# Head norms run inside the next mixer's projection; Hyena's weights, filter taps and one DeltaNet load are rearranged

## The reference, cut to what matters

```python
def head_rmsnorm(o, w, n_heads):
    b_, l_, hd = o.shape
    oh = o.reshape(b_, l_, n_heads, hd // n_heads)
    oh = oh * lax.rsqrt(jnp.mean(oh * oh, axis=-1, keepdims=True) + EPS)
    return oh.reshape(b_, l_, hd) * w.astype(F32)
# GLA and DeltaNet: y = head_rmsnorm(o, norm_w, 4) * silu(og)
# Mamba:            y = head_rmsnorm((o + xs * d) * silu(z), norm_w, 4), then back to row-major order

def hyena_filters(l_, w1, b1, w2, b2, w3, b3, w4, freq):
    ...                                         # feats: (1024, 33)
    h = jnp.sin(f[0] * (feats @ w1 + b1))       # 64 wide
    h = jnp.sin(f[1] * (h @ w2 + b2))
    h = jnp.sin(f[2] * (h @ w3 + b3))
    h = h @ w4                                  # 1024 wide: 2 orders x 2 directions x 256 channels
    ...
    return h.reshape(l_, HY_ORDER, N_DIR, D_GROUP) * window[:, None, None, :]
```

## Time and profile before

| | us |
|---|---|
| median of 3 runs (2051.81 to 2055.04) | 2052.24 |
| the profiled execution | 2053.32 |
| its span in the trace | 2051.5 |
| PE busy | 1722.3 (84% of the span) |
| DVE busy | 1141.3 (56%) |
| ACT busy | 850.6 (41%) |
| POOL busy | 363.4 (18%) |
| TensorE clock granted, mean | 0.908 of full |

### The profile page before, as it was taken

One profiled execution on the slowest core, in us unless ns is written; L12 is line 12 of the kernel. 1 busy time (PEld: TensorE's weight loads), 2 busy tenths in 40 slices (PEclk: granted clock), 3 DMA queues, 4 the chain that ended last, 5 costly groups with the idle time before them and its releaser, 6 DMA issues. The chain is left out here.

```text
span 2051.5 us, 20519 instructions
## 1 busy us (share of the span) xinstructions
PE 1722.3 (84%) x7806; PEld 1228.2 (60%) x7806; DVE 1141.3 (56%) x1325; ACT 850.6 (41%) x1115; POOL 363.4 (18%) x455
## 2 busy tenths in 40 slices
PE   5898979975897849969899888970999999999981
PEld 2453745465455638954335656860888888888860
DVE  3621842268224535654323343337888888888874
ACT  4112224311224626632200003431777777777752
POOL 0000310031000578300041342430010101010100
PEclk9899989988898869979879999985999999999996
DMA  9620200020000733320142024213999999999955
GB/s 370 237 100 1 83 0 0 0 83 1 0 1 4 243 119 99 104 81 0 42 128 103 0 82 155 69 54 156 368 381 400 383 399 379 402 383 403 379 218 184
DMA packets 105706, 338.26 MB, mean 165 GB/s; under 512 B 35050, under 2 KB 44829, under 8 KB 80905
## 3 DMA queue, kind: packets, MB, share of 16 engines
q1 hardware_dynamic: 97024, 314.28, 40.4%
q0 software_dynamic: 4608, 16.78, 3.3%
q10 hardware_dynamic: 3977, 5.90, 1.0%
HBM read 303.83 MB, written 33.09 MB: 164 GB/s over the span
## 5 line engine op out<-in xcount | busy, mean ns | idle before, releaser
L2842 DVE TENSOR_TENSOR w_lo<-w_raw,w_hi 128x2048 fp32r<-128x2048 f32 x192 | 438.4, 2291 | 66.0 <-ACT w_hi L2788 66.0
L2788 ACT ACTIVATE w_hi<-w_raw 128x2048 fp32r<-128x2048 f32 x192 | 368.0, 1917 | 143.6 <-PE ps L2744 134.9
L489 PE MATMUL ps<-hT,w_mixer 128*128 128x512 f32 (+1 forms) x768 | 311.2, 566 | 5.6 <-PEq L186 4.7
L489 PEld LDWEIGHTS ps<-hT,w_mixer 128*128 128x128 f32 x768 | 146.8, 193 | 161.4 <-issue 158.1
L2742 PE MATMUL ps<-w_hi,xsT_hi 128*128 128x512 f32 x512 | 203.1, 397 | 2.4 <-DVE xsT_lo L2847 2.4
L2744 PE MATMUL ps<-w_hi,xsT_lo 128*128 128x512 f32 x512 | 200.5, 392 | 0.0
L2743 PE MATMUL ps<-w_lo,xsT_hi 128*128 128x512 f32 x512 | 200.4, 391 | 0.0
L2717 POOL DMA_INDIRECT moe_sum<-y,idx_col x16 | 32.0, 1998 | 490.6 <-ACT y L2808 490.6
L2742 PEld LDWEIGHTS ps<-w_hi,xsT_hi 128*128 128x128 f32 x512 | 96.8, 189 | 22.1 <-DVE xsT_lo L2847 2.8
L2744 PEld LDWEIGHTS ps<-w_hi,xsT_lo 128*128 128x128 f32 x512 | 96.7, 189 | 20.5
L2743 PEld LDWEIGHTS ps<-w_lo,xsT_hi 128*128 128x128 f32 x512 | 96.8, 189 | 19.4
(11 more groups left out here) (473 smaller groups left out, 2990.1 us busy)
## 6 DMA issues: line engine op xcount, KB each, us to landing
w_raw<-in_moe_w_gate SPq DMA_DIRECT2D x64, 1024.0 KB, 6.8
w_raw<-in_moe_w_up SPq DMA_DIRECT2D x64, 1024.0 KB, 8.6
w_raw<-in_moe_w_down SPq DMA_DIRECT2D x64, 1024.0 KB, 8.5
w_mod_row<-in_w_mod SPq DMA_DIRECT2D x32, 512.0 KB, 5.1
w_mod<-in_w_mod SPq DMA_DIRECT2D x8, 1024.0 KB, 14.5
w_mixer<-in_w_in SPq DMA_DIRECT2D x4, 2048.0 KB, 10.6
dn_ma<-dn_ma SPq DMA_DIRECT2D x16, 512.0 KB, 3.3
dn_mT<-dn_ma SPq DMA_DIRECT2D x20, 256.0 KB, 3.7
```

The lines of the kernel that those rows point to most:

```text
L489: last = nc.tensor.matmul(S.ps[:, 3 * (i % 2) + c, 0:n], S.w[:, k, b["col"]:b["col"] + P], S.hT[:, k, t0:t0 + n], start=(k == 0), stop=(k ...
L2788: nc.scalar.activation(wh[q % RING][:, :], S.raw[q % RAW][:, :], ACT.Copy).then_inc(s.hi, 1)
L2842: nc.vector.tensor_tensor(wl[q % RING][:, :], S.raw[q % RAW][:, :], wh[q % RING][:, :].bitcast(F32), ALU.subtract).then_inc(s.lo, 1)
```

## The change

The three head norms are no longer stages. `HeadNorm` gives its pieces to the next `project_conv`: ACT's silu and root come first on ACT, DVE's chain comes first on DVE, POOL's multiplication after the memsets, and PE's 16 transposes come after block 0 of the projection, into four banks of their own, with ACT's four copies after its copies of block 0. PE waits for a bank's copy before it writes that bank again (`free`). `o` and the squares lie in parts of `yT` that are not yet in use, so that the next mixer's buffers don't overlap them.

Hyena's weights are no longer loaded beside the norm of DeltaNet but at the start of `hy_c`, in four transfers of two row groups each, and PE's first product waits for them one at a time. The filter layers are computed twice, on partitions 0 to 63 and 64 to 127, and `w4` is split between the two halves, so that the two tap matmuls of a token tile read different halves of the array's rows. One DVE instruction multiplies both orders by the window (128x1024), DVE takes the sum and POOL only the difference, each 128x512; the window comes in four transfers; the table `hy_fwd` is waited for only by the stage that reads it. In DeltaNet, `dn_a` ends after 8 small loads; the other 8 are issued at the start of `dn_s`. Fewer stages move the two clearings of semaphores from before `dn_c` and `hy_c` to before `dn_l` and `hy_f`.

```diff
-def project_conv(nc, S, A, name, blocks, plan, ctx=True, side=None):
+def project_conv(nc, S, A, name, blocks, plan, norm, ctx=True, side=None, weights=None):
...
+            if weights:
+                col, n = weights
+                src = A["w_in"][0, :, col:col + n].rearrange("(p k) n -> p k n", p=P)
+                for j in range(4):
+                    sp.dma_start(S.w[:, 2 * j:2 * j + 2, 0:n], src[:, 2 * j:2 * j + 2, :]).then_inc(s.w_in[j], 16)
...
             last.then_inc(s.zeroed, 1)
+            norm.pool(s, pool)
...
                 if n >= 2:
                     pe.wait_ge(s.tok_e, n - 1)
+                norm.free(s, pe, 6 + n % 2)
...
-            pe.wait_ge(S.w_ready, S.w_count)
+            if not weights:
+                pe.wait_ge(S.w_ready, S.w_count)
...
+                    if i >= 1:
+                        norm.free(s, pe, 3 * (i % 2) + c)
                     for k in range(KD):
+                        if weights and i == 0 and c == mine[0][0] and k % 2 == 0:
+                            pe.wait_ge(s.w_in[k // 2], 16)
                         last = nc.tensor.matmul(S.ps[:, 3 * (i % 2) + c, 0:n], S.w[:, k, b["col"]:b["col"] + P],
...
                     to_tokens(pe, i - 1)
+                if i == 0:
+                    norm.pe(s, pe)
                 if side:
...
         def _(act):
+            norm.act(s, act)
             act.wait_ge(s.zeroed, 1)
...
                     nc.scalar.activation(d, src, ACT.Copy).then_inc(s.evac, 1)
+                if i == 0:
+                    norm.act_out(s, act)
...
+            norm.dve(s, dve, ch)
             for i, b in enumerate(blocks):
...
+    def pe(self, s, pe):
+        S = self.S
+        pe.wait_ge(s.nsq, 1)
+        for g in range(4):
+            kb, half = g // 2, g % 2
+            for t in range(4):
+                last = self.nc.tensor.transpose(S.ps[:, self.banks[g], t * P:(t + 1) * P],
+                                                self.o[:, half * 4 + t, kb * P:(kb + 1) * P], S.t("ident"))
+            last.then_inc(s.ntr, 1)
+
+    def free(self, s, pe, bank):
+
+        if bank in self.held:
+            pe.wait_ge(s.cp, self.held.pop(bank))
...
-            for st in range(2):
-                for d in range(2):
-                    load_blocks(sp, st, d)
+            for d in range(2):
+                load_blocks(sp, 0, d)
...
                 sp.wait_ge(ma_st[b], stored(b, N))
+            for d in range(2):
+                load_blocks(sp, 1, d)
             for st in range(2, T):
...
-            sp.wait_ge(s.tables, 6 * 16)
+            sp.wait_ge(s.tables, 4 * 16)
...
+                for q in range(2):
+                    r = slice(q * side.HF, (q + 1) * side.HF)
+                    last = nc.tensor.matmul(S.ps[:, 2 + 2 * (lt % 3) + q, :], h[r, lt * P:(lt + 1) * P], w4[r, :],
+                                            start=True, stop=True)
+                last.then_inc(s.taps, 1)
...
+                nc.vector.tensor_tensor(hs[:, lt, :, :], x[:, :, 0, :], x[:, :, 1, :], ALU.add).then_inc(s.sums, 1)
...
-                nc.gpsimd.tensor_tensor(hs[:, lt, q, :], tap[i % 2][:, 0, :], tap[i % 2][:, 1, :], ALU.add)
-                nc.gpsimd.tensor_tensor(hd[:, lt, q, :], tap[i % 2][:, 0, :], tap[i % 2][:, 1, :], ALU.subtract
-                                        ).then_inc(s.sd, 1)
+                nc.gpsimd.tensor_tensor(hd[:, lt, :, :], x[:, :, 0, :], x[:, :, 1, :], ALU.subtract).then_inc(s.diffs, 1)
```

More of the change, by code:

```diff
@@ L436, in project_conv @@
     with Stage(nc, name, "zeroed prod evac centre conv_ch conv_done tok_t tok_e cm_done "
-                         + (side.sems if side else "")) as s:
+                         + (side.sems if side else "") + norm.sems + (" w_in*4" if weights else "")) as s:
         line = [plan.take(f"{name}_line{b}", [P, 1284]) for b in range(2)]
@@ L1098, in mamba @@
     small = plan.at
-    o = plan.take("mb_o", [P, LT, DG])
+    yT_block = lambda k, name, shape: Plan(nc, S.yT_at + k * SEQ * 4, S.hT_at).take(name, shape)
+    o = yT_block(2, "mb_o", [P, LT, DG])
     mark = plan.at
@@ L1110, in mamba @@
                            tok=z[:, :, b * P:(b + 1) * P], latents=True))
-    project_conv(nc, S, A, "mb_c", blocks, Plan(nc, small), side=gates)
+    project_conv(nc, S, A, "mb_c", blocks, Plan(nc, small), norm, side=gates)
     plan.at = mark
@@ L2180, in hyena @@
                            by_parity=True))
-    side = FilterLayers(nc, A, Plan(nc, mark + 3 * 2 * 1284 * 4 + 96))
+    side = FilterLayers(nc, A, Plan(nc, S.norm_end))
     side.ps = S.ps
-    project_conv(nc, S, A, "hy_c", blocks, plan, ctx=False, side=side)
-    assert plan.at <= side.at
+    project_conv(nc, S, A, "hy_c", blocks, Plan(nc, SBUF_END - 384 - CONV_BYTES), norm, ctx=False, side=side,
+                 weights=(HY0, HY_COLS))
+    assert side.end <= SBUF_END - 384 - CONV_BYTES
     h, w4 = side.h, side.w4
@@ L2191, in hyena @@
     late = Plan(nc, SBUF_END - 2 * 2 * SEQ * 4)
-    with Stage(nc, "hy_f", "win_in tables taps tapped zeroed sd") as s:
+    fwd_in = nc.alloc_semaphore("hy_fwd_in")
+    with Stage(nc, "hy_f", "win_in*4 tables taps tapped zeroed sums diffs") as s:
         win = plan.take("hy_window", [P, LT, DG])
-        tap = [plan.take(f"hy_taps{b}", [P, 2, DG]) for b in range(2)]
+        tap = [plan.take(f"hy_taps{b}", [P, 2, 2, DG]) for b in range(2)]
         assert plan.at <= side.at
@@ L2202, in _ @@
         def _(sp):
-            sp.dma_start(win[:, :, :], A["window"].rearrange("(t p) c -> p t c", p=P)).then_inc(s.win_in, 16)
+            rows = A["window"].rearrange("(t p) c -> p t c", p=P)
+            for i in range(4):
+                sp.dma_start(win[:, 2 * i:2 * i + 2, :], rows[:, 2 * i:2 * i + 2, :]).then_inc(s.win_in[i], 16)
             for b in range(2):
@@ L3012, in _ @@
                 nc.vector.memset(S.ones[:, :], 1.0)
-        for stage in stages:
-            stage(nc, S, A)
+        modulate(nc, S, A)
+        norm = gla(nc, S, A)
+        norm = mamba(nc, S, A, norm)
+        norm = deltanet(nc, S, A, norm)
+        hyena(nc, S, A, norm)
+        project_out(nc, S, A)
+        experts(nc, S, A)
+        finish(nc, S, A)
         with Stage(nc, "end", "") as s:
```

228 lines of the change are left out of this document (109 added, 119 removed).

## The result

| | before | after |
|---|---|---|
| median of 4 runs on one chip, us | 2052.17 (2051.81 to 2055.04) | 1996.59 (1994.66 to 1997.96) |
| ratio, 95% interval | | 0.9724 (0.9708 to 0.9739) |
| span of the profiled execution, us | 2051.5 | 1996.1 |
| PE busy, us | 1722.3 | 1700.3 |
| mean granted clock of TensorE | 0.908 | 0.924 |

The change saves 55.6 us. The kernel was run again for the experiments: 1997.25 (ratio 0.9718, 0.9701 to 0.9734) and 1993.63 (0.9715, 0.9700 to 0.9730).

A forecast was written before the change was run, and what follows sets the result against it. PE bounds projections and taps; in the three norm stages one engine works at a time. 14.9 + 20.3 + 11.2 - 2.3 + 3.7 + 7.8 = 55.6 us off 2053.3 gives 1997.7, stated as 1997, range 1989 to 2006.

The forecast's parts named there:

- taps: Hyena's tap stage: 2.1 us a tile, 16.8 for eight, stage 22.5 instead of 30.27 us; gain 7.8, ends 0 and 11.
- GLA's norm: GLA's norm beside Mamba's projection: PE starts 17.0 us earlier, transposes cost 2.1; gain 14.9 us.
- Mamba's norm: Mamba's norm beside DeltaNet's projection: PE starts 22.4 us earlier, transposes cost 2.1; gain 20.3 us.
- DeltaNet's norm, weights in quarters: DeltaNet's norm beside Hyena's projection: 18.2 us earlier, less 4.9 for the first weight quarter and 2.1 for transposes; gain 11.2.
- clearings: Both semaphore clearings remain, at other stages, so 2 x 1.15 = 2.3 us counted as removed is lost again.
- small loads: End of DeltaNet's matrices' stage: eight of SP's 16 small-load issues leave it; gain 3.7 us, other end 0.
- the rival: Hyena's projection: all weight quarters land together, PE starts at 10.8 us rather than 4.9; 6 us more, 2003; chance 7%.
- The question of the port: Tap stage: whether DVE's sum or POOL's difference goes first; DVE first, as taken, 2.1 us a tile, POOL first 3.4.
- The rivals at 2003 and 2005: 2003: Hyena's weight quarters land together, 7%. 2005: taps gain nothing, half-row matmuls not overlapping or POOL first, 13%.
- the clock at 1.00 from the start of DeltaNet's and Hyena's projections: Rival: clock stays up without PE's pause, saving up to 3 us in Hyena's projection, 1.2 in DeltaNet's; 1993; chance 8%.
- a clock below 1.00 in the middle of one: Rival: PE loses the clock without rest in the projections; 2092 if Hyena's alone ran at 1.2 GHz; chance 2%.
- Two of the prediction's signs: Right: taps' stage at 22 to 23 us. Wrong: any stage before 267 or after the taps differing by over 1 us.

## Why the prediction was right, step by step

The forecast was 1997 us, the median 1996.59. That it came within half a microsecond is luck: the taps gained 2.7 us more than forecast and GLA's norm 1.5 us less. The steps, from the timelines:

| step | predicted | measured |
|---|---|---|
| GLA's norm | 14.9 | 13.4 |
| Mamba's norm | 20.3 | 20.5 |
| DeltaNet's norm, weights in quarters | 11.2 | 11.2 |
| clearings | -2.3 | -2.5 |
| small loads | 3.7 | 3.8 |
| taps | 7.8 | 10.5 |
| sum | 55.6 | 56.9 |

The table of starts gives 57.3 us from GLA's scan to `hy_k`, so 0.4 is in none of these steps. The span gains 55.4, since the changed kernel's profiled execution was 1.4 us late before any of it and 0.5 is lost at the end.

**GLA's norm.** From the start of the scan's last sum to PE's projection it was 17.74 us and is 0.75: 17.0, as predicted. The transposes cost 1.9 rather than 2.1, in all three projections. What the sum did not have is the clock. Block 0 took 18.95 us instead of 17.3. The windows of the profiled execution, and then of another one of the same kernel:

```profile
268.00:270.00 2.00, 1.62 (x5) 1.35 (x6) 1.67 (x2) 1.64 (x2) 0.27 (x6) 0.66 0.03 8
270.00:272.00 2.00, 2.00 (x6) 1.64 (x5) 1.97 (x2) 1.98 (x2) 0.37 (x1) 0.50 0.00 0
272.00:274.00 2.00, 2.00 (x9) 1.52 (x9) 1.58 (x3) 1.31 (x3) 2.00 (x1) 0.98 0.00 0
```

```profile
268.00:270.00 2.00, 2.00 (x11) 1.77 (x10) 1.97 (x2) 1.99 (x2) 0.00 (x0) 1.00 0.03 8
270.00:272.00 2.00, 2.00 (x9) 1.38 (x8) 2.00 (x1) 1.98 (x2) 1.13 (x1) 1.00 0.00 0
```

In the first the clock falls to 0.50 for some 3 us although PE is at dense work; in the second it stays at 1.00 and block 0 takes 17.27. In the last 6 us or so before the projection PE was busy for about three quarters of the time in both, at a clock of 1.00. Of ten profiled executions whose projection starts with block 0, four show the fall (18.85 to 18.95 us) and six don't (17.26), whatever the edit elsewhere. So the step is 15.1 in one kind of execution and 13.4 in the other, and the prediction's 14.9 is the first kind. What decides between them I did not find. Nor is the loss always one of the whole: two of the four with the fall reach DeltaNet's projection 222.3 us after Mamba's, as the six without it do (222.0 to 222.7), because the clock stays at 1.00 almost to the end of Mamba's scan; the other two take 224.4 and 224.8.

**Mamba's norm.** 22.4 us between the scan's end and PE, as predicted, less 1.9. The chain took 15.6 us from the stage's start, as predicted, and block 0 16.1 instead of 16.84, so the cover was 0.5 us instead of 1.2; it held in each execution read.

**Hyena's projection.** The first quarter's landing was the uncertain term: 4.9 predicted, 5.1 measured, and PE waited once. The weights in two show what the rival would have cost (7 us, not the 6 that I gave it).

**Clearings.** PE's pause before `dn_l` is 2.29 us and was 1.05, before the taps 7.19 and was 5.94: 1.24 and 1.25 us.

**Taps.** The step that was mis-sized. The period of a tile was to be 2.1 us, from a product of at most 1.38 and a sum of 0.6 with waits between; it was 1.86, from 1.22 and 0.69 with waits too short to show (8 x 0.24 = 1.9 us of the difference). The double product costs less than two single ones. The window's first quarter was there after 2.7 us, not 4.1 (1.4 us more); the memset and POOL's last difference gave 0.6 back. The question of the port went as I had taken it: DVE's sum, 0.69, runs at its own length, and POOL's eight differences take 1.70 to 1.78 us each, where POOL needs 1.26 in the kernel with the sums on POOL. The Trainium skill (SBUF — State Buffer, section "Who interferes with whom") says that a DVE instruction with two SBUF inputs holds up a GpSimd one that reads SBUF, and one with a single SBUF input, outside its two-port modes, doesn't. The trace agrees with both halves: 0.5 us more for POOL beside the sum, nothing beside the product that reads PSUM.

The rivals at 2003 and 2005 did not occur. Neither did the clock at 1.00 from the start of DeltaNet's and Hyena's projections, nor a clock below 1.00 in the middle of one. Two of the prediction's signs came out against it: the taps' stage took 19.8 us and not 22 to 23, and GLA's scan, ahead of the change, began 1.4 us later in the profiled execution (0.2 us earlier in another one, so that this is no effect of the change).

## What to carry to other kernels

A stage in which one engine works for 12 to 16 us costs PE all of it, and vanishes beside the next stage's dense matmuls if its chain is shorter than the first block that does not need it; compare these two times, with the block at the clock that PE has there. The order in PE's program decides: the same pieces ahead of block 0 gave 34 of 57 us back. Count the issues of a DMA queue at the end of a stage, each of 0.46 us, and move those whose data are read later. After a wait is taken away, look at what lies just behind it before building on the gain: here it was 0.5 us away.

## What the runs showed of the hardware

Two float32 matmuls on 64 rows each, on different halves of the array, take 1.13 us together at a clock of 1.00, and 2.08 at 0.50, each pair standing alone. These are pairs of the kernel with the sums on POOL:

```profile
979.60 1.13 PE L2252 MATMUL ps<-hy_fw,hy_h 64*128 64x512 f32 x4 [1.71 <-DVE hy_taps L2265]
...
984.48 2.08 PE L2252 MATMUL ps<-hy_fw,hy_h 64*128 64x512 f32 x4 [0.36 <-DVE hy_taps L2265]
```

On the same half, back to back at 0.50, a pair takes 3.41.

In the taps' stages the share of time in which PE is busy does not tell the granted clock. With both taps on one half, PE was busy all the time and got 0.50 (the 1.2 GHz level); with the two halves it was busy for 2.44 and 2.26 of 4 us and had 1.00 (2.4 GHz); where POOL let it have a tile only every 2.44 us, the clock was 1.00 at first (975 to 979) and then fell back to 0.50. Why, no run shows. Windows of the kernel on one half, of the changed kernel, and of the one with the sums on POOL:

```profile
980.00:990.00 10.00, 10.00 (x13) 4.01 (x12) 5.75 (x6) 0.00 (x0) 5.08 (x4) 0.50 1.07 368
```

```profile
974.00:976.00 2.00, 2.00 (x10) 0.85 (x6) 1.21 (x1) 0.00 (x0) 0.00 (x0) 0.70 1.07 351
976.00:980.00 4.00, 2.44 (x12) 0.69 (x8) 3.77 (x6) 0.00 (x0) 3.10 (x2) 1.00 1.02 284
980.00:984.00 4.00, 2.26 (x8) 0.60 (x8) 3.93 (x5) 0.00 (x0) 3.82 (x3) 1.00 1.18 292
```

```profile
983.00:987.00 4.00, 3.20 (x8) 0.50 (x4) 2.45 (x2) 0.00 (x0) 4.00 (x4) 0.50 1.04 376
987.00:991.00 4.00, 0.00 (x0) 0.00 (x0) 1.69 (x2) 0.00 (x0) 4.00 (x4) 0.50 1.05 389
```

In the changed kernel the clock of 1.00 leaves PE idle for 0.73 us before each pair, so DVE sets the time. Whether PE would set it at 0.50 is not shown: the two pairs that start 1.84 us apart there are just under DVE's 1.86.

Executions differ in a stretch through memory: from the issue of the transposed matrices' loads to the write of the inverse's last piece, code that no edit here touches, it took 10.2 to 16.0 us (11.8, 13.1 and 11.0 in the three of the changed kernel itself). Of the 5.3 us between two profiled executions of the changed kernel (spans 1996.1 and 1990.8), 0.8 arose before Mamba's projection, 2.0 between it and DeltaNet's, where the clock's fall is 1.7, and 1.2 in the stages with this stretch. What moves them stays open.
